# Stick phase of a hybrid attention step: the gate piece whole between the two turns of keys, and the weighted values ahead of the scores

## What is computed

```python
z = jnp.einsum('bqhd,bshd->bhqs', q, k).astype(jnp.float32) * (d ** -0.5)
causal = (k_pos[None, :] < q_pos[:, None])[None, None]
log_beta = jax.nn.log_sigmoid(z)
log_rest = jnp.where(causal, jax.nn.log_sigmoid(-z), 0.0)
suffix = lax.cumsum(log_rest, axis=3, reverse=True) - log_rest
A = jnp.where(causal, jnp.exp(log_beta + suffix), 0.0)
return jnp.einsum('bhqs,bshd->bqhd', A.astype(v.dtype), v)
...
gate = jax.nn.sigmoid(gm.reshape(gm.shape[:-1] + (N_BRANCH, D_MODEL)))
```

## Time and profile before

| | before |
|---|---|
| median of 3 runs | 3098.61 us (3094.63 to 3100.53) |
| the profiled execution | 3091.68 us |
| its span | 3090.0 us |
| TensorE busy | 2896.4 us, 94% of the span |
| VectorE busy | 1513.3 us, 49% |
| GpSimd busy | 1147.8 us, 37% |
| ScalarE busy | 1004.6 us, 33% |
| granted TensorE clock, mean | 0.975 of full speed |

### The profile page before, as it was taken

One profiled execution on the slowest core, in us unless ns is written; L12 is line 12 of the kernel. 1 busy time (PEld: TensorE's weight loads), 2 busy tenths in 40 slices (PEclk: granted clock), 3 DMA queues, 4 the chain that ended last, 5 costly groups with the idle time before them and its releaser, 6 DMA issues. The chain is left out here.

```text
span 3090.0 us, 50524 instructions
## 1 busy us (share of the span) xinstructions
PE 2896.4 (94%) x20331; PEld 2384.9 (77%) x20331; DVE 1513.3 (49%) x2135; ACT 1004.6 (33%) x1843; POOL 1147.8 (37%) x1001
## 2 busy tenths in 40 slices
PE   6899999999989999989998999899988996999798
PEld 5788888888877888867776777677766776877686
DVE  7232221100004777666766676567657774333333
ACT  6441211111113444434443444334435662000221
POOL 4242331111104445445544545345535563433100
PEclk9899999999999999999999999999998998999899
DMA  6543332212216554665466545754448348444443
GB/s 215 178 154 114 131 123 68 79 68 71 73 66 215 171 162 156 223 214 176 159 215 217 185 159 175 240 189 159 150 153 229 126 128 238 165 169 163 163 143 109
DMA packets 383015, 485.98 MB, mean 157 GB/s; under 512 B 27888, under 2 KB 241904, under 8 KB 382416
## 3 DMA queue, kind: packets, MB, share of 16 engines
q1 hardware_dynamic: 341200, 359.32, 36.9%
q0 software_dynamic: 34688, 111.05, 9.6%
q10 hardware_dynamic: 6912, 12.59, 1.2%
HBM read 359.28 MB, written 123.60 MB: 156 GB/s over the span
## 5 line engine op out<-in xcount | busy, mean ns | idle before, releaser
L376 PE MATMUL prj_bank<-hidden_hi,w_hi 128*128 128x512 f32 (+2 forms) x1360 | 490.9, 361 | 13.1 <-DVE w_lo L439 13.1
L378 PE MATMUL prj_bank<-hidden_hi,w_lo 128*128 128x512 f32 (+2 forms) x1360 | 487.1, 358 | 0.0
L377 PE MATMUL prj_bank<-hidden_lo,w_hi 128*128 128x512 f32 (+2 forms) x1360 | 486.8, 358 | 0.0
L1100 POOL TENSOR_TENSOR stk_beta<-stk_beta,stk_left 128x1024 f32<-128x1024 f32 (+4 forms) x160 | 275.8, 1724 | 549.2 <-DVE stk_left L1017 549.2
L809 PE MATMUL stk_g_bank<-hidden_hi,w_hi 128*128 128x512 f32 (+2 forms) x928 | 351.1, 378 | 14.6 <-PEq L62 10.8
L811 PE MATMUL stk_g_bank<-hidden_hi,w_lo 128*128 128x512 f32 (+2 forms) x928 | 336.6, 363 | 0.0
L810 PE MATMUL stk_g_bank<-hidden_lo,w_hi 128*128 128x512 f32 (+2 forms) x928 | 335.8, 362 | 0.0
L376 PEld LDWEIGHTS prj_bank<-hidden_hi,w_hi 128*128 128x128 f32 x1360 | 256.9, 189 | 44.8 <-DVE w_lo L439 13.3
L378 PEld LDWEIGHTS prj_bank<-hidden_hi,w_lo 128*128 128x128 f32 x1360 | 256.7, 189 | 32.5
L377 PEld LDWEIGHTS prj_bank<-hidden_lo,w_hi 128*128 128x128 f32 x1360 | 257.0, 189 | 31.3
L1017 DVE TENSOR_TENSOR_SCAN stk_left<-stk_rest,stk_left 128x513 f32<-128x513 f32 x192 | 244.6, 1314 | 8.1 <-ACT stk_rest L965 8.0
(11 more groups left out here) (254 smaller groups left out, 5460.2 us busy)
## 6 DMA issues: line engine op xcount, KB each, us to landing
stk_kd<-in_cache_sb_k SPq DMA_DIRECT2D x64, 1024.0 KB, 5.4
stk_vd<-in_cache_sb_v SPq DMA_DIRECT2D x64, 1024.0 KB, 7.3
w_raw<-in_w_in SPq DMA_DIRECT2D x112, 512.0 KB, 3.8
scratch_zT<-stk_g_out POOLq DMA_DIRECT2D x72, 256.0 KB, 2.3
mrg_gate<-scratch_zT SPq DMA_DIRECT2D x24, 768.0 KB, 4.4
scratch_zT<-prj_z POOLq DMA_DIRECT2D x48, 256.0 KB, 2.3
prj_w<-in_w_in SPq DMA_DIRECT2D x18, 512.0 KB, 3.9
mrg_u_raw<-scratch_uT SPq DMA_DIRECT2D x9, 1024.0 KB, 9.2
```

The costliest lines, as they stand in the source:

```text
L376: pe.matmul(out, w_hi[u][:, k, :], hi[:, k, :], start=k == 0, stop=False)
L377: pe.matmul(out, w_hi[u][:, k, :], lo[:, k, :], start=False, stop=False)
L378: last = pe.matmul(out, w_lo[u][:, k, :], hi[:, k, :], start=False, stop=k == KC - 1)
L1100: pool.tensor_tensor(bt, bt, left[prompts.index(n) % 2][:, :, 1:keys + 1], ALU.mult).then_inc(a_done, 1)
```

## The change

In a step that turns keys and holds a gate piece, the piece is no longer cut into two halves, one between the first turn and `turn_a` and one behind the second turn: all of it stands between the first turn and `turn_a`. In a step that turns no keys the piece stays where it was, last. In every step `add_o` now stands ahead of `scores`.

```diff
@@ -812,14 +812,9 @@
                 if k1 == KC:
                     last.then_inc(g_summed, 1)
 
-            def gates_part(s, half):
+            def gates_piece(s):
                 if s < len(share) and share[s]:
-                    p, k0, k1 = share[s]
-                    mid = (k0 + k1) // 2 if s + 1 in kblocks else k0
-                    if half == 0 and mid > k0:
-                        gates(p, k0, mid)
-                    if half == 1:
-                        gates(p, mid, k1)
+                    gates(*share[s])
 
             def turn_k(n, half):
                 if n not in kblocks:
@@ -915,16 +910,18 @@
             turn_k(0, 0)
             turn_k(0, 1)
             for s in range(N + LAG_O):
+                if s >= LAG_O:
+                    add_o(s - LAG_O)
                 if s < N:
                     scores(s)
-                if s >= LAG_O:
-                    add_o(s - LAG_O)
                 turn_k(s + 1, 0)
-                gates_part(s, 0)
+                if s + 1 in kblocks:
+                    gates_piece(s)
                 if 0 <= s - LAG_T < N:
                     turn_a(s - LAG_T)
                 turn_k(s + 1, 1)
-                gates_part(s, 1)
+                if s + 1 not in kblocks:
+                    gates_piece(s)
             for p, k0, k1 in rest_of_gates:
                 gates(p, k0, k1)
```

## The result

The changed kernel takes 3192.52 us (median of 4 runs, 3191.41 to 3197.07), the kernel before 3099.39 on the same chip (3094.63 to 3100.53). The ratio is 1.0302, with a 95% interval of 1.0289 to 1.0315: 3.0% slower, 93 us. The forecast was 3160 us, slower, with 3112 to 3200 as its range.

A forecast was written before the change was run, and what follows sets the result against it. TensorE, busy 94% of the span, was taken as the bound. Terms 56 + 15 + 5 - 3 - 5 - 5 = 63 us on the 3098.6 median gave 3162, stated as 3160 us; range 3112 to 3200.

The forecast's parts named there:

- `add_o` two steps on: Two steps behind a key step with a piece, `add_o` waits for VectorE's take behind its scan: 56 us in all.
- step 81's: `add_o` two steps behind key step 79: reached 3.63 us after the second turn, startable at 5.12, so waiting 1.5 us.
- The step after that: One step later without a piece, VectorE is still behind and TensorE waits again: ten places, 15 us, bounds nothing to 35.
- the other order by itself: `add_o` ahead of scores loses the scores' 1.12 us of cover where it stands close behind a take: 5 us.
- waits replaced: Existing waits at `add_o` and turns of weights where a new, longer wait takes their place: -5 us.
- The clock falls too: Rival, chance 0.11: new TensorE waits lower the granted clock, adding 20 to 45 us, for 3180 to 3210.
- The gains: Second turns behind a piece no longer find VectorE late, -3 us; mask-product scores lead to `add_o` more cheaply, -5 us.
- Uniting the halves: Whole piece between the turns: 5.64 us against 5.86 for two halves, offset by a dearer turn ahead of `add_o`; nothing left.
- step 79: The key step with a gate piece whose TensorE and VectorE timelines were read as standing for most key steps.
- The signs: Expected in the profile after: 45 to 60 `add_o` waits, 50 to 80 us; VectorE idle +2.9 us per second key copy.
- tile changes: Switches between tile shapes on TensorE outside mask products: taken as even, bound of 20 us either way over 230 steps.

The follow-up runs named there:

- The early scan: Changed kernel with VectorE's scan, in key steps that hold a piece, moved ahead of the second key copy: 3099.98 us, 1.0009; same edit in kernel before: 3090.48 us.
- an eighth of the piece: Changed kernel with the last 3 of a piece's 24 matmuls behind the second turn of keys: 3160.12 us, 1.0216.
- a quarter: Changed kernel with the last 6 of a piece's 24 matmuls behind the second turn of keys: 3139.15 us, 1.0141.
- neither part of the change: Two runs: kernel before with `add_o` ahead of scores, piece still halved, 3121.48 us; changed kernel with scores first again, piece whole between the turns, 3159.09 us.
- The order alone: Kernel before with `add_o` ahead of scores in every step, the piece still cut in halves: 3121.48 us, 1.0081.
- the cut: GpSimd makes the low part of the gate weights for one of eight row blocks only: changed kernel 3156.07 us, 1.0200; kernel before 3084.16 us, 0.9955.

## Why the prediction was right, and where its sum fell short

The direction and the mechanism held, and the time is in the range. The sum was 63 us against 93. By its steps:

- **"`add_o` two steps on", 56 us: right.** Forecast +5.12 us from second turn to `add_o`, measured +5.13; forecast wait 1.5, measured 1.49. In the changed kernel 37 such places make 52.5 us, where I had counted 39. The early scan takes these waits away, an eighth of the piece shortens step 81's to 0.79 and a quarter to 0.1, and neither part of the change brings them alone: shown.
- **"The step after that", 15 us, and "the other order by itself", 5 us: mis-sized.** All other waits at `add_o` come to 94.1 - 52.5 = 41.6 us against 6.3 before, 35 more, where 20 had been forecast and 5 were taken off for waits replaced. Of these, 6.5 us are step 68's, with 3.9 us gone at its scores. The order alone shows that the greater part belongs to the order and not to the piece: 30.2 us three steps on. I had given the order by itself 5 us, and had not looked for the places where a scan that GpSimd holds up was still covered by the scores. There are as many long scans as before: 12 decode scans of over 2.5 us then, 10 now, none with the cut in either kernel. The cut takes 19 us of waits at `add_o` away in the changed kernel. So held scans and the lost cover make this part together. The mean decode scan also grows, from 1.84 to 2.22 us, by the other meeting with GpSimd told above; what that adds is open.
- **"The clock falls too", given 0.11 and nothing in the sum: it happened in part.** I took stretches of 25 us over the stick phase, each times what its granted clock lacks to 1.00. They add up to 30 us before and to 49 in the changed kernel, with 18 stretches under the full clock in place of 8. Stretches of 4 us around step 79 (start:end, length, busy time by engine, granted clock, DMA):

```profile
1410.00:1414.00 4.00, 2.82 (x44) 1.58 (x47) 3.97 (x7) 3.12 (x5) 0.63 (x1) 1.00 0.69 222
1414.00:1418.00 4.00, 2.56 (x42) 1.84 (x33) 4.00 (x4) 1.09 (x2) 3.98 (x3) 1.00 0.30 110
1418.00:1422.00 4.00, 2.39 (x12) 1.45 (x12) 4.00 (x7) 0.00 (x0) 1.89 (x3) 0.59 0.62 174
1422.00:1426.00 4.00, 4.00 (x16) 3.38 (x15) 0.81 (x2) 2.54 (x3) 1.08 (x1) 0.55 0.79 285
1426.00:1430.00 4.00, 4.00 (x19) 3.29 (x18) 0.00 (x0) 0.00 (x0) 0.00 (x0) 1.00 0.00 0
```

  TensorE is busy for 2.82 and 2.56 of 4 us, standing still for 1.18, 0.38 and then 2.67 us. In the next two stretches the clock is 0.59 and 0.55, near the lower of its levels of 1.2 and 2.4 GHz. What I had held against this rival, a stretch of 225 us at 1.00, has only 1.05 us of standing still in it, and so says nothing on waits like these. Two more kernels point at the waits of about 2.5 us: with the product of GpSimd cut, where few of them are left, the same sum is back at 30 us; with a quarter of the piece behind, where they stand and those of 1.49 us are gone, it is 52 us (the order alone: 37). That the clock follows these waits is read from rows; no run changed the clock alone.
- **The gains, -3 and -5 us: right, the second a little larger.** The four waits of second turns behind a piece are gone, 3.1 us. The scores that end in a mask product take 0.10 us less ahead of a turn (0.79 against 0.89 for 256 columns), 64 times, and 0.07 at 8 new-key units: 7 us. The other blocks, each timed to the start of the next, take the same in either order within 0.01 us (a block of scores in 64-row tiles 1.13, `add_o` 1.01 to 1.03). Uniting the halves I had put at nothing; no run shows it by itself.
- **The signs.** VectorE's idle time ahead of key copies grew by 2.8 us a step (forecast 2.9), its scan ended 4.90 us behind the second turn (4.89), and second turns wait some 10 us for VectorE, all in steps without a piece. The waits at `add_o` are more than said: 62 and 94 us, against 45 to 60 and 50 to 80.
- **Account of the span's 105 us:** waits at `add_o` +88, the clock up to +19, other waits some +5, tile changes -7.
- **The range.** It held in part by luck. I had made it wide for tile changes of up to 20 us either way, which hardly moved; the clock, which I had left out of the sum, took up that room.

## What to carry to other kernels

A hand-over is a point at which one engine waits for what another has made. When TensorE's work is moved across one, look at what the other engine has behind that hand-over in its own list: here the take of a sum stood behind a scan, and the scan behind a copy that waits for the moved turn. The time between hand-over and use has to cover that whole list, and here it could be read from one trace to a hundredth of a microsecond (5.12 us forecast, 5.13 measured). If idle time lies ahead of the hand-over, move the waiting engine's own work there before TensorE's. And where work is moved ahead of a wait that is short, ask what had kept it short: step 79's scan was held up for as long before, and cost 0.47 us then and 2.67 now. What an instruction collides with moves too.

## What the runs showed of the hardware

VectorE's scans wait for GpSimd's products of two tensors. The decode scan of step 79 in the changed kernel started at 1415.85 and took 3.53 us, undisturbed 1.28. GpSimd at that time:

```profile
1415.92 2.36 POOL L1082 TENSOR_TENSOR w_lo<-w_raw,w_hi 128x1024 fp32r<-128x1024 f32 x1
```

The scan ended 1.10 us behind the end of this product at 1418.28, nearly a whole scan's length. In the changed kernel no decode scan without such a product beside it took over 1.29 us. The Trainium skill says so (SBUF — State Buffer, SBUF: two separate sides: an exclusive lock on the shared port pair, held for the whole instruction, for a VectorE operation with two inputs in SBUF against a GpSimd operation that reads SBUF), and the trace agrees: 3.53 us is about 2.4 + 1.1. Which of the two began first the rows don't show, their recorded starts are 0.07 us apart.

Around step 79 the granted clock fell when TensorE had stood still for at most 2.67 us at a time, and eight transposes then took 1.62 us in place of 0.85. It fell as well behind a wait of 1.76 us for a take, at 1199.41, and stayed at 1.00 behind the 1.49 us of step 81, at 1436.24. Stretches of 4 us of the changed kernel, columns as above:

```profile
1196.00:1200.00 4.00, 2.24 (x22) 1.16 (x22) 4.00 (x8) 2.30 (x4) 0.73 (x1) 1.00 0.79 262
1200.00:1204.00 4.00, 4.00 (x29) 3.33 (x26) 3.08 (x4) 1.49 (x2) 3.98 (x3) 0.57 0.11 37
...
1434.00:1438.00 4.00, 2.51 (x30) 1.92 (x28) 4.00 (x6) 1.30 (x3) 1.91 (x1) 1.00 0.87 321
1438.00:1442.00 4.00, 4.00 (x22) 3.08 (x21) 3.90 (x5) 1.94 (x2) 3.98 (x4) 1.00 0.17 66
```
